# Rebuilding the prologue of a hybrid GLA / conv / pool block: sums of squares, modulation weights, context blocks

## The reference, cut to what matters

```python
def modulate(x, w, shift, scale):
    return rmsnorm(x, w) * (1 + scale) + shift

def adaln(cvec, w_mod, b_mod, n):
    m = jax.nn.silu(cvec) @ w_mod[:, : n * D_MODEL] + b_mod[: n * D_MODEL]
    return jnp.split(m, n, axis=-1)
...
        sh1, sc1, g1, sh2, sc2, g2 = [m[:, None, :] for m in adaln(c, w_mod[l], b_mod[l], N_MOD)]
        h = modulate(x, norm1_w[l], sh1, sc1)
        proj = h @ w_in[l]
...
            csh1, csc1 = adaln(c_ctx, w_mod[l], b_mod[l], 2)
            hc = modulate(xc, norm1_w[l], csh1, csc1)
            pc = hc @ w_in[l][:, K_OFF:R_OFF]
```

## Time and profile before

| what | value |
|---|---|
| median of 3 runs | 1096.13 us (1095.15 to 1096.31) |
| the profiled execution | 1095.63 us |
| its span in the trace | 1093.8 us |
| TensorE busy | 1070.4 us, 98% of the span |
| VectorE, ScalarE, GpSimd busy | 826.0, 508.9, 305.8 us |

### The profile page before, as it was taken

The page is one execution under the profiler, slowest core; times in us unless marked ns, Lnnn a source line. Parts: engine busy times, 40 slices in busy tenths (PEclk is TensorE's granted clock), DMA queues, the critical chain, the costliest instruction groups (busy, mean ns, idle before and its releaser), DMA issues.

```text
span 1093.8 us, 15383 instructions
## 1 busy us (share of the span) xinstructions
PE 1070.4 (98%) x5064; PEld 864.4 (79%) x5064; DVE 826.0 (76%) x1070; ACT 508.9 (47%) x818; POOL 305.8 (28%) x280
## 2 busy tenths in 40 slices
PE   8999999999999999999999999999999999999996
PEld 4578888877888888787888888888778888888884
DVE  4877869636534998699878777787987778777776
ACT  5646533365623312576766666666422222222234
POOL 1000006386301264003232332323332222222323
PEclk9999999999999999999999999999999999999998
DMA  9523331001013566215867666677747844864604
GB/s 367 224 97 115 115 116 40 23 36 39 21 39 116 201 209 241 79 60 222 314 233 265 233 243 261 227 269 277 290 171 279 316 186 191 344 243 186 261 1 154
DMA packets 58896, 199.74 MB, mean 183 GB/s; under 512 B 5600, under 2 KB 6880, under 8 KB 58336
## 3 DMA queue, kind: packets, MB, share of 16 engines
q1 hardware_dynamic: 58848, 199.11, 48.4%
HBM read 139.32 MB, written 59.77 MB: 182 GB/s over the span
## 4 chain that ended last, share of the span: by engine, by line
PE 49%; DVE 4%; issue 0%; DVEq 0%; ACT 0%
PE ob L1363 13%; PE main L1405 13%; PE sm L1363 10%; PE sm L1405 8%; PE ob L1405 6%; DVE XR L2612 1%; DVE XR L2679 1%; DVE stage L2493 1%; DVE slot L2443 0%; DVE slot L2438 0%; DVE stage_last L2493 0%; DVE t_tmp L2486 0%; DVE hid L2500 0%; DVE t_tmp L2477 0%; DVE t_tmp L2472 0%
## 5 line engine op out<-in xcount | busy, mean ns | idle before, releaser
L945 PE MATMUL main<-a_hi,w_hi 128*128 128x512 f32 x376 | 125.7, 415 | 0.0
L1363 PE MATMUL ob<-h_sum,slot 128*128 128x512 f32 x504 | 122.9, 393 | 2.2 <-DVE hid L2500 2.1
L1819 ACT ACTIVATE slot<-raw 128x512 fp32r<-128x512 f32 x80 | 50.2, 631 | 153.1 <-PE main L1405 58.4
L945 PE MATMUL main<-a_lo,w_hi 128*128 128x512 f32 x376 | 116.6, 391 | 0.0
L945 PE MATMUL main<-a_hi,w_lo 128*128 128x512 f32 x376 | 116.2, 390 | 0.0
L1363 PEld LDWEIGHTS ob<-h_sum,slot 128*128 128x128 f32 x504 | 95.5, 190 | 22.9 <-issue 2.5
L2612 DVE SCALAR_TENSOR_TENSOR XR<-main,mods,XR 128x512 f32<-128x512 f32 x112 | 83.3, 748 | 28.8 <-PE main L1405 27.8
L945 PEld LDWEIGHTS main<-a_hi,w_lo 128*128 128x128 f32 x376 | 70.6, 188 | 15.6
L945 PEld LDWEIGHTS main<-a_lo,w_hi 128*128 128x128 f32 x376 | 70.6, 188 | 15.5
L945 PEld LDWEIGHTS main<-a_hi,w_hi 128*128 128x128 f32 x376 | 66.8, 188 | 17.8 <-issue 5.8
L1405 PE MATMUL main<-t_even,slot 128*128 128x512 f32 x336 | 78.1, 389 | 0.0
(11 more groups left out here) (354 smaller groups left out, 2495.0 us busy)
## 6 DMA issues: line engine op xcount, KB each, us to landing
hidden_kept<-stage SPq DMA_DIRECT2D x98, 512.0 KB, 4.3
raw<-wstream SPq DMA_DIRECT2D x60, 512.0 KB, 4.2
t_even<-hidden_kept SPq DMA_DIRECT2D x56, 512.0 KB, 5.6
raw<-wstream SPq DMA_DIRECT2D x16, 1024.0 KB, 5.6
stage<-hidden_kept SPq DMA_DIRECT2D x21, 512.0 KB, 5.4
stage_last<-hidden_kept SPq DMA_DIRECT2D x21, 512.0 KB, 6.2
wmod<-wm SPq DMA_DIRECT2D x4, 2048.0 KB, 23.4
mbuf<-wm SPq DMA_DIRECT2D x16, 512.0 KB, 4.1
```

Of the source, the lines that this page charges most:

```text
L945: ins = pe.matmul(main[:, bank, half * HALF:(half + 1) * HALF], w[:, slot, k, :], x[:, half * HALF:(half + 1) * HALF], start=begin, stop=end)
L1363: ins = pe.matmul(hid_bank(acc, odd), slots1[j][:, w, kp, :], parts[x][:, kp, :], start=PARTS[j][3] and kp == 0 and m == 0, stop=kp == KP ...
L1819: act.activation(slots2[j][:, 0, :, :, :], operand(s, j), ACT.Copy).then_inc(w2_hi, 1)
```

## The change

The diff does the following.

- **Squares.** Blocks 0 and 1 are summed by TensorE as they are; blocks 2 and 3, 4 and 5, 6 and 7 are added in pairs by VectorE first (three additions, the last in two pieces) and TensorE sums each pair. New semaphore `sums1_read` frees the buffers.
- **Modulation weights.** Eight transfers of 1 MB, one for each block, instead of four of 2 MB; a piece on the DRAM side is 1 KB long. SyncE waits for the square of block j before it issues transfer j. Rows and turned rows are now eight jobs of half the width, with four groups instead of three.
- **Context.** The context part of every block goes to GpSimd: it scales by `rs1` (`scale_context`), ScalarE scales and shifts once into `c_hi` and once in place, GpSimd subtracts (`context_low`). GpSimd also splits the first weight tile into `w_hi` and `w_lo`, which ScalarE and VectorE did.
- **Latent part.** VectorE keeps the 1024 latent columns of each block; block 0 is done in two halves.
- **TensorE's order.** `modulation_rows(k + 2)` stands before `gate_part(k)`, `modulation_turned(k + 2)` behind it, and `value_part(k)` follows in the same round, so that after `gate_part(7)` there is one value part. Fillers are 9, 1 and 1 instead of 18 and 2. High products of `gate_part` wait for high parts alone.

```diff
...
-GROUPS = 3
+GROUPS = 4
...
-SQ_ADDED = (1, 2, 3, 5, 6)
...
-SMALL = [(_name, _j) for _j in range(KT // 2) for _name in ("rows", "turn")]
+SMALL = [(_name, _j) for _j in range(KT) for _name in ("rows", "turn")]
...
-        wmod = [at(f"wmod{j}", [P, KT, HALF], F32, HA + place * KIB) for j, place in enumerate((0, 32, 16, 48))]
...
-        SUM_FIRST = {0: acc1, 4: acc1b}
-        def sq_place(k):
-            return SQ_ADDED.index(k) if k in SQ_ADDED else len(SQ_ADDED)
+        def square_place(k):
+            return (acc1[:, :], acc1b[:, :], sq1[:, 0, :], sq1[:, 1, :], acc1[:, :], acc1b[:, :], sq1[:, 1, :], sq1[:, 0, :])[k]
+        def ab_ready(k):
+            return small_freed(S_OF[("turn", k)])
...
             def load_wmod(j):
-                sp.dma_start(wmod[j][:, :, :].rearrange("p k c -> p (k c)"), wm1[j]).then_inc(wmod_loaded[j], 16)
+                sp.wait_ge(sq1_made, j + 1)
+                sp.dma_start(wmod[j][:, :, :], wm1[j // 2].rearrange("p (k j c) -> p k j c", j=2, c=2 * P)[:, :, j % 2, :]
+                             ).then_inc(x_wmod_loaded[j], 16)
...
             sp.dma_start(xs[:, :, N:NA], ct).then_inc(ctx_loaded, 16)
             for k in range(KT):
-                sp.dma_start(xs[:, k, 0:N], xt[k]).then_inc(x_loaded[k], 16)
+                sp.dma_start(xs[:, k, 0:N], xt[k]).then_inc(x_wmod_loaded[k], 16)
             load_wmod(0)
             sp.dma_start(wg[:, :, :].rearrange("p k c -> p (k c)"), wg_in).then_inc(wg_loaded, 16)
+            load_wmod(1)
             load_tile(0)
-            load_wmod(1)
-            load_wmod(2)
-            load_wmod(3)
+            for j in range(2, KT):
+                load_wmod(j)
             sp.dma_start(gw[:, :, :].rearrange("r h c -> r (h c)"), gw_in).then_inc(gw_loaded, 16)
             sp.dma_start(small[:, NFIRST:NSMALL], small_in[:, NFIRST:NSMALL]).then_inc(masks_loaded, 16)
             for t in range(1, 4):
                 load_tile(t)
             sp.wait_ge(h1_lo, KT)
+            sp.wait_ge(c1_lo, KT)
...
+            def scale_context(k):
+                pool.tensor_tensor(xs[:, k, N:NA], xs[:, k, N:NA], rs1[:, N:NA], ALU.mult).then_inc(c1_scaled, 1)
+            def context_low(k):
+                pool.wait_ge(c1_hi, k + 1)
+                pool.tensor_tensor(c_lo[:, k, :], xs[:, k, N:NA], c_hi[:, k, :].bitcast(F32), ALU.subtract).then_inc(c1_lo, 1)
+            pool.wait_ge(rs1_made, 3)
+            scale_context(0)
+            scale_context(1)
+            pool.wait_ge(raw_loaded[0], 16)
+            pool.tensor_tensor(w_hi[:, 0, :, :], raw[:, 0, :, :], ones.unsqueeze(1).broadcast_to([P, KT, P]),
+                               ALU.mult).then_inc(hi_made, 1)
+            context_low(0)
+            pool.wait_ge(hi_made, 1)
+            pool.tensor_tensor(w_lo[:, 0, :, :], raw[:, 0, :, :], w_hi[:, 0, :, :].bitcast(F32),
+                               ALU.subtract).then_inc(split_done, 1)
+            for k in range(2, KT):
+                scale_context(k)
+                context_low(k - 1)
+            context_low(KT - 1)
...
                     pe.wait_ge(*small_freed(s - 2))
-                pe.wait_ge(wmod_loaded[j], 16)
...
@@ -1007,7 +1034,7 @@
             def keep_busy(count):
                 for _ in range(count):
-                    pe.matmul(sm[:, 0, 0:NFIRST], ones, small[:, 0:NFIRST], start=True, stop=True)
+                    pe.matmul(main[:, 0, 0:NFIRST], ones, small[:, 0:NFIRST], start=True, stop=True)
...
+            both_halves = (1, 0)
+            pe.wait_ge(sq1_made, 1)
+            sums_of(square_place(0), both_halves, True, True, False).then_inc(sums1_read, 1)
+            pe.wait_ge(sq1_made, 2)
+            sums_of(square_place(1), both_halves, True, False, False).then_inc(sums1_read, 1)
+            pe.wait_ge(acc1_made, 1)
+            sums_of(square_place(2), both_halves, True, False, False).then_inc(sums1_read, 1)
+            pe.wait_ge(acc1_made, 2)
+            sums_of(square_place(4), both_halves, True, False, False)
             pe.wait_ge(acc1_made, 3)
-            sums_of(acc1, (0, 1), True, True, False)
-            keep_busy(FILL[1])
-            pe.wait_ge(acc1_made, len(SQ_ADDED))
-            sums_of(acc1b, (1,), True, False, False)
-            pe.wait_ge(sq1_made, KT)
-            sums_of(sq1[:, (KT - 1) % 2, :], (1,), True, False, True).then_inc(sums1_done, 1)
-            sums_of(acc1b, (0,), False, False, False)
-            sums_of(sq1[:, (KT - 1) % 2, :], (0,), False, False, True).then_inc(sums1_done, 1)
+            sums_of(square_place(7), (1,), True, False, True).then_inc(sums1_done, 1)
+            pe.wait_ge(acc1_made, 4)
+            sums_of(square_place(7), (0,), False, False, True).then_inc(sums1_done, 1)
             modulation_rows(0)
             modulation_turned(0)
             modulation_rows(1)
+            keep_busy(FILL[1])
             modulation_turned(1)
...
+            keep_busy(FILL[1])
...
             def gate_part(k):
-                pe.wait_ge(h1_lo, k + 1)
...
+                pe.wait_ge(h1_hi, k + 1)
+                pe.wait_ge(c1_hi, k + 1)
+                if k < KT - 1:
+                    highs()
+                    lows()
                 else:
...
+                    lows()
+                    highs().then_inc(tile_done, 1)
...
+                if k == 0:
+                    pe.wait_ge(hi_made, 1)
+                first_product_of(k, 1, slice(0, P), [(w_hi[:, 0, k, :], a_hi, c_hi), (w_hi[:, 0, k, :], a_lo, c_lo)], last=False)
                 if k == 0:
                     pe.wait_ge(split_done, 1)
-                ins = first_product_of(k, 1, slice(0, P), [(w_hi[:, 0, k, :], a_hi, c_hi), (w_hi[:, 0, k, :], a_lo, c_lo),
-                                                           (w_lo[:, 0, k, :], a_hi, c_hi)])
+                ins = first_product_of(k, 1, slice(0, P), [(w_lo[:, 0, k, :], a_hi, c_hi)], first=False)
...
             gate_part(0)
+            modulation_rows(2)
             value_part(0)
-            modulation_rows(2)
-            gate_part(1)
             modulation_turned(2)
-            value_part(1)
-            modulation_rows(3)
-            gate_part(2)
-            value_part(2)
-            modulation_turned(3)
-            for k in range(3, KT):
+            for k in range(1, KT - 1):
+                if k + 2 < KT:
+                    modulation_rows(k + 2)
                 gate_part(k)
-                if k >= 4:
-                    value_part(k - 1)
+                if k + 2 < KT:
+                    modulation_turned(k + 2)
+                value_part(k)
+            gate_part(KT - 1)
             value_part(KT - 1)
             gate_products(0)
...
+                act.wait_ge(x_wmod_loaded[k], 16)
+                if k in (4, 5, 7):
+                    act.wait_ge(sums1_read, {4: 1, 5: 2, 7: 3}[k])
+                elif k == 6:
+                    act.wait_ge(acc1_made, 1)
+                act.activation(square_place(k), xs[:, k, :], ACT.Square).then_inc(sq1_made, 1)
...
+                act.wait_ge(*ab_ready(k))
...
+                    for half in (1, 0):
+                        cols = slice(half * HALF, (half + 1) * HALF)
+                        act.wait_ge(x_scaled, 2 - half)
+                        ins = act.activation(a_hi[:, k, cols], xs[:, k, cols], ACT.Identity, bias=ab1[:, k, 0:1],
+                                             scale=ab1[:, k, 2:3])
+                        if half == 1:
+                            copy_rows(1)
+                    ins.then_inc(h1_hi, 1)
                 else:
-                    act.activation(a_hi[:, k, :], xs[:, k, 0:N], ACT.Identity, bias=ab1[:, k, 0:1])
-                    act.activation(c_hi[:, k, :], xs[:, k, N:NA], ACT.Identity, bias=ab1[:, k, 1:2]).then_inc(h1_hi, 1)
-                if k in COPY_AT:
-                    copy_rows(COPY_AT[k])
+                    act.wait_ge(x_scaled, k + 3)
+                    act.activation(a_hi[:, k, :], xs[:, k, 0:N], ACT.Identity, bias=ab1[:, k, 0:1]).then_inc(h1_hi, 1)
+                act.wait_ge(c1_scaled, k + 1)
+                act.activation(c_hi[:, k, :], xs[:, k, N:NA], ACT.Identity, bias=ab1[:, k, 1:2], scale=ab1[:, k, 3:4])
+                act.activation(xs[:, k, N:NA], xs[:, k, N:NA], ACT.Identity, bias=ab1[:, k, 1:2],
+                               scale=ab1[:, k, 3:4]).then_inc(c1_hi, 1)
+                if k + 2 < KT:
+                    copy_rows(k + 2)
...
+            def modulation(k):
+                s = S_OF[("turn", k)]
                 dve.wait_ge(small_done, s + 1)
...
+                ts(ab1[:, k, 2:4], sm[:, s % 2, 2:4], mods[:, 0, k:k + 1], one_col("n1", k), ALU.add, ALU.mult)
+                ts(ab1[:, k, 0:2], sm[:, s % 2, 0:2], one_col("bmod", k), None, ALU.add).then_inc(small_free[s % 2], 1)
+                dve.wait_ge(*ab_ready(k))
+            dve.wait_ge(sq1_made, 4)
+            tt(square_place(2), square_place(2), square_place(3), ALU.add).then_inc(acc1_made, 1)
```

(30 more changed lines are left out.)

124 lines of the change are left out of this document (25 added, 99 removed).

## The result

| | before | after |
|---|---|---|
| median of 5 runs | 1096.13 us (1094.78 to 1096.31) | 1099.46 us (1098.84 to 1101.6) |
| profiled execution, its span | 1095.63, 1093.8 | 1098.84, 1097.0 |
| first gate part over | 35.15 | 32.41 |
| gate tile over (end of gate part 7) | 61.87 | 65.45 |
| first gate product starts | 65.38 | 68.96 |

The ratio is 1.0035, with a 95% interval of 1.0024 to 1.0047: slower by 3.8 us (2.6 to 5.2; the medians differ by 3.3, the two profiled executions by 3.2), against a forecast of 1099.2 in a range of 1093.6 to 1102.6. The first gate product moved by +3.58; the sum of the prediction was +3.55.

A forecast was written before the change was run, and what follows sets the result against it. TensorE, busy 98% of the span, was taken as the bound, with time winnable only in the prologue. -2.75 + 1.8 - 0.95 + 3.7 + 1.75 = +3.55 on 1095.63 gave 1099.2 us, range 1093.6 to 1102.6.

The forecast's parts named there:

- Start, -2.75: Up to the first gate part: over at 32.4 instead of 35.15 us, with VectorE and GpSimd contending; -4.7 without contention.
- named it for a sign: At the start, in the new profile: VectorE's `low1(0)` at over 2 us would show the forecast right.
- Own work, +1.8: TensorE behind the first gate part: six half-width jobs of rows and turned rows, 9.0 us against 7.2; +0.9 to +3.6.
- -0.95: First gate part to first gate product: TensorE's waiting in the kernel before, taken out and replaced by newly laid-out waits.
- Waits in the blocks, +3.7: TensorE's waits on GpSimd and VectorE at blocks 0 and 3 to 7; from 0.3 without contention to 6.
- the pair of VectorE and GpSimd sets the pace: At blocks 6 and 7: the two engines need 3.8 us a block, TensorE 2.9; waits of 1.6 and 0.2.
- Gate tile, +1.75: Behind gate part 7: one value part instead of two covers the 3.5 us chain to the first gate product.
- What was to cost nothing: Prologue: eight transfers, SyncE's waits, ScalarE's work, the pads' masks, and fewer fillers if the clock stays at 2.4 GHz.
- The premise of a shift: Behind the first gate product: whatever moves its start at 65.38 us moves the kernel's end by as much.
- The forecast's own range: Whole kernel: +2 to +6, 1097.5 to 1101.8 us, from rows at 0.9 to 1.35 and block waits at 2.5 to 5.

The follow-up runs named there:

- split_back: Changed kernel with the first weight tile split on ScalarE and VectorE again, context still on GpSimd; ratio to the kernel before 1.0019.
- vector_all: Changed kernel with the first weight tile split on ScalarE and VectorE and the context scaling and low parts on VectorE; ratio to the kernel before 1.0035.
- late_values: Changed kernel with the value parts of the last blocks one block late again; ratio to the kernel before 1.0047.
- values_at_once: Kernel before, with each value part right behind its gate part from block 3 on; ratio to the kernel before 1.0004.
- short_context: split_back with GpSimd's context instructions cut to 16 of 256 columns; ratio to the kernel before 1.0000.
- three_groups: Changed kernel with three groups of modulation rows instead of four; ratio to the kernel before 1.0049.
- split_fill6: split_back with six filler products ahead of the sums of squares instead of nine; ratio to the kernel before 1.0024.
- early_tile: split_fill6 with the first weight tile's transfer, high part and low part moved earlier; ratio to the kernel before 1.0027.
- four_groups: Kernel before with four groups in the modulation rows instead of three, jobs as wide as before; ratio to the kernel before 0.9998.
- groups_busy: Kernel before with four groups and one filler product behind each of modulation rows 0 and 1; ratio to the kernel before 0.9986.
- context_vector: Changed kernel with the context's scaling and low parts on VectorE, first weight tile still split on GpSimd; ratio to the kernel before 1.0084.

## Why the prediction was right, point by point

**Start, -2.75.** Measured -2.74, and the mechanism is shown by split_back: VectorE and GpSimd took turns. That the number fits to 0.01 is luck, for two things in it came out otherwise. The roots were to come 0.7 earlier and did not: the first logarithm stands at 22.72, where before had 22.54. Nine filler products lasted 8.61 us, to 11.73, the first sum waited for them, and ScalarE then waited 0.32 and 0.88 for sums. That cost 0.9 against the forecast. What made it good was that GpSimd's context piece came earlier than laid out: I had let VectorE's shift go ahead of `w_hi`, and GpSimd went first. So it was that shift that took over 2 us (2.76), and not `low1(0)` as I had named it for a sign (1.53).

**Own work, +1.8, and -0.95.** Measured are six jobs of 1.00 + 0.36 = 8.2 against 7.2, so +1.0; the jobs came out at the cheap end. But a value part behind turned rows takes 1.92 and not 1.75 (43.64 to 45.56), and eight value and seven gate parts sum to 23.3, not 22.05. The two errors nearly cancel: 31.5 against 31.05.

**Waits in the blocks, +3.7.** Measured 3.1: 0.66 and 0.33 at gate part 1, 0.27, 0.06 and 0.31 at gate parts 3, 4 and 5, 1.21 and 0.29 at 6 and 7. The size was right and the places partly: gate part 1 was missing, since I had not followed `w_lo` into the scaling of block 1, and at gate parts 3 to 5 came 0.64 where I had laid out 1.7. There GpSimd was let in between two VectorE instructions instead of being passed over. The Trainium skill, on the page "SBUF — State Buffer", section "Who interferes with whom", says that whoever issues first keeps the shared pair for its whole instruction; in the rows of 49 to 51 us above the trace agrees, and my reading of the earlier trace rows, that GpSimd is passed over, was too strict.

The reason that I gave for the end, that the pair of VectorE and GpSimd sets the pace at blocks 6 and 7, was right only from the last turned rows on. VectorE was no bottleneck before them: it waited 0.43, 1.86, 1.20 and 1.86 for TensorE's turned rows of blocks 4 to 7. The wait of 1.21 at gate part 6 is for `a_lo(6)`, which stands in VectorE's list behind the modulation and scaling of block 7, and these need turned rows that TensorE makes only behind gate part 5. Of the 1.21, turns with GpSimd are 0.49. The waits were also less often for GpSimd itself than I expected: its `c_lo` came last at gate parts 1, 3 and 5 (0.33, 0.27 and 0.31, which is 0.9 of the 3.1), and the rest was for ScalarE at gate part 1 and for VectorE. In vector_all, without any turns, it is 36.74 from the first gate part to the gate product, against 36.55 in the kernel after: the forecast number for these waits would have come out about as well with VectorE doing all of it.

**Gate tile, +1.75.** Measured 1.9 of idle time. The number was right and the words "hangs on nothing uncertain but the order" were wrong. Putting the order back won nothing (late_values, where a half clock took about 1.5), and alone in the kernel before it costs 1.0 (values_at_once). In the changed kernel and six of its variants (late_values, split_back, short_context, three_groups, split_fill6, early_tile) the gate product comes 5.08 to 5.20 after VectorE has made `a_lo(7)` (5.31 and 5.36 in the two with the context on VectorE). The waits at blocks 6 and 7 and the open chain are one chain; I had counted them as two terms, each of which could be mended. What leads it is in the part on late_values: the turned rows of block 7, then VectorE's list.

**What was to cost nothing.** All bytes moved as forecast, no job of rows waited for its weights behind the first gate part, and the tile order cost nothing as long as the roots were late. The clock did cost: not in the profiled execution of the changed kernel (mean granted clock 0.996, and the fastest of its five), but in those of five other kernels. The four other executions of the changed kernel show 0.991 to 0.993, and before had 0.995 in its profiled one. So part of the 3.8 us is probably clock; where it fell in them no trace shows.

**The premise of a shift.** From the first gate product to the end of the span it is 1028.4 before and 1028.0 after; over all fourteen kernels 1027.4 to 1030.7, all but one within 1.1 of before. The premise holds to about a microsecond, and so no experiment here can show differences smaller than that in the time alone.

**The range.** The forecast's own range does not follow from its terms: rows between 0.9 and 1.35 and waits between 2.5 and 5 give +1.45 to +6.65, 1097.1 to 1102.3, and not +2 to +6. Nothing in the result hangs on it.

**In sum.** The prediction was right in its number and in its main mechanism, the turns of VectorE and GpSimd at the start; that the sum fits to 0.03 is luck, since terms were off by more and cancelled. Of the +3.6, taking the weight tile off GpSimd gives back about 1.8, and taking the length out of its context pieces another 1.7 to 2.1. Together that is about the whole loss; the earlier start and the dearer blocks then cancel. Three shares stay open: the half-width jobs, which cost TensorE 1.0; the order of value parts, which costs 1.0 when alone, both partly beside waits; and a rival that no run tested, the place of the jobs of rows. Before, the turned rows of blocks 6 and 7 were there by 49.9 (49.08 + 0.81 until the next matmul); now those of block 7 come at 57.98, just ahead of their use, and VectorE waits for them.

## What to carry to other kernels

When work goes to an idle engine, ask what it shares with the engine it relieves: here the small context pieces cost a little less than on VectorE, and the weight split, two pieces of 2.4 us on GpSimd against 1.0 and 1.2 elsewhere, cost 1.8 on the path. Before pricing an order change at the end of a stage, find the one instruction from which the next stage has a constant distance, ask what that instruction itself waited for, and ask whether the change moves it. A wait of one to two microseconds on TensorE can cost more behind it than in it: the change to four groups, with no measurable effect alone, became a gain of 2.2 us with three filler products in its waits. Before crediting an edit with what two traces differ by, compare a point ahead of the edit, here the first logarithm.

## What the runs showed of the hardware

- **The clock.** It fell to half behind waits of 1.76 (late_values), 1.12 and 0.46 (four_groups), 0.32 and 0.98 (groups_busy) and 0.40 and 1.24 (three_groups), and within one of 4.73 (context_vector), for 3 to 10 us. It did not fall in the profiled execution of the changed kernel behind 0.40 and 1.62, nor behind the 1.76 ahead of the gate product, nor in before behind 0.69, 0.57 and 0.77. So such a wait is a risk and not a fixed price.
- **One input is enough.** VectorE's TENSOR_SCALAR with a single tensor in SBUF (1024 columns in 0.81) took 2.76 under GpSimd's product. I had expected turns only for instructions with two. The Trainium skill, on the page "SBUF — State Buffer", section "Who interferes with whom", lists `tensor_scalar` among the operations that can take the shared pair in their fast modes; the trace agrees that it contends, and which mode it ran in no row shows.
- **Short pieces are not cheap on GpSimd.** Cut to 16 of 256 columns, its scalings still took 0.47 and its subtractions 0.68 on average (0.73 for 256 columns alone): 0.2 to 0.34 where VectorE left it alone, 0.95 to 1.23 where it did not.
- **Fillers vary.** The first 18 filler products took 12.69 to 13.88 us in five kernels with the same code there, the nine of the changed kernel 7.49 to 8.61 in its variants. In before-like kernels the sums start right behind them, so this alone moves the prologue by up to a microsecond from one execution to the next; in split_back it was 0.56 of what looked like the edit's gain.
